# Four context pieces, and the context mixer moved to stand directly ahead of the state-space mixer

## What is computed

```
x   = macaron_ffn(x,   mod[:, 0:3],     *ffn1)      # main:    "ffn_4"
ctx = macaron_ffn(ctx, mod_ctx[:, 0:3], *ffn1)      # context: the pieces "ctx_a", "ctx_b", ...
h_ctx_f, h_ctx_b = context_states(ctx, ...)         # "ctx_mix"
x, _, _ = mix_sublayer(x, ..., h_ctx_f, h_ctx_b, ...)   # "ssd"
x = macaron_ffn(x, mod[:, 6:9], *ffn2)              # "ffn_5"
```

## Time and profile before

| | |
|---|---|
| median of 3 executions | 1648.93 us |
| the profiled execution's own time | 1650.2 us |
| its span, first to last instruction | 1648.4 us |
| TensorE busy | 1639.3 us (99%), 8804 matmuls |
| VectorE busy | 1249.4 us (76%) |
| ScalarE busy | 938.4 us (57%) |
| mean granted TensorE clock | 0.999 |

### The profile page before, as it was taken

How to read it: one execution, slowest core, us unless ns; L and a number is a source line. 1 busy time by engine, 2 the same in 40 slices (tenths; PEclk the granted TensorE clock), 3 DMA queues, 4 the chain that set the end, 5 groups by cost and what they waited for, 6 DMA issues and landing times.

```text
span 1648.4 us, 23158 instructions
## 1 busy us (share of the span) xinstructions
PE 1639.3 (99%) x8804; PEld 1417.2 (86%) x8804; DVE 1249.4 (76%) x1672; ACT 938.4 (57%) x1418; POOL 218.9 (13%) x368
## 2 busy tenths in 40 slices
PE   9999999999999999999999999999999999999998
PEld 7888889888888888888888888889888889988887
DVE  6888776788978877688788878779665669986564
ACT  6655567655565554565456546557655558664543
POOL 1100100001414000014005010122001012310000
PEclk9999999999999999999999999999999999999999
DMA  8977553687868687757658788674566545357551
GB/s 283 340 269 254 169 184 119 238 297 263 270 209 280 233 311 256 258 185 236 211 181 287 256 281 284 212 236 146 182 226 238 203 134 198 107 186 237 187 196 64
DMA packets 105342, 366.89 MB, mean 223 GB/s; under 512 B 13840, under 2 KB 14352, under 8 KB 105232
## 3 DMA queue, kind: packets, MB, share of 16 engines
q1 hardware_dynamic: 92736, 334.73, 59.6%
q0 software_dynamic: 12352, 30.61, 5.7%
q10 hardware_dynamic: 144, 0.07, 0.0%
HBM read 357.95 MB, written 2.17 MB: 218 GB/s over the span
## 4 chain that ended last, share of the span: by engine, by line
PE 91%; DVE 4%; DMA 2%; ACT 1%; issue 1%; SPq 0%; DVEq 0%; POOLq 0%; POOL 0%; ACTq 0%
PE dn L650 29%; PE gu L605 13%; PE tp L605 13%; PE gu L561 11%; PE gu L612 7%; PE tp L612 7%; PE dn L576 3%; DMA raw<-in_weights 2%; DVE w_lo L1958 1%; PE gu L589 1%; PE tp L589 1%; PE dn L605 1%; DVE w_lo L1951 1%; PE dn L561 1%; PE dn L612 1%
## 5 line engine op out<-in xcount | busy, mean ns | idle before, releaser
L1958 DVE TENSOR_TENSOR w_lo<-raw,w_hi 128x1024 fp32r<-128x1024 f32 x518 | 631.1, 1232 | 286.3 <-ACT w_hi L1261 283.5
L1261 ACT ACTIVATE w_hi<-raw 128x1024 fp32r<-128x1024 f32 x520 | 547.1, 1055 | 439.7 <-PE gu L612 153.4
L650 PE MATMUL dn<-w_hi,actT_hi 128*128 128x512 f32 x616 | 240.7, 391 | 0.0
L650 PE MATMUL dn<-w_hi,actT_lo 128*128 128x512 f32 x616 | 239.8, 389 | 0.0
L650 PE MATMUL dn<-w_lo,actT_hi 128*128 128x512 f32 x616 | 239.8, 389 | 0.0
L605 PE MATMUL tp<-hT,w_hi 128*128 128x512 f32 x928 | 232.2, 391 | 0.0
L605 PE MATMUL gu<-hT,w_hi 128*128 128x512 f32 x944 | 225.2, 389 | 0.3 <-DVE hT L1966 0.3
L561 PE MATMUL gu<-w_hi,hT 128*128 128x512 f32 x672 | 209.4, 393 | 0.9 <-DVE w_lo L1951 0.5
L605 PEld LDWEIGHTS gu<-hT,w_hi 128*128 128x128 f32 x944 | 177.0, 188 | 37.2 <-DVE hT L1966 0.6
L605 PEld LDWEIGHTS tp<-hT,w_hi 128*128 128x128 f32 x928 | 170.5, 188 | 32.9
L561 PEld LDWEIGHTS gu<-w_hi,hT 128*128 128x128 f32 x672 | 124.4, 188 | 27.5 <-DVE hT L1966 1.3
(11 more groups left out here) (367 smaller groups left out, 2028.0 us busy)
## 6 DMA issues: line engine op xcount, KB each, us to landing
raw<-in_weights SPq DMA_DIRECT2D x561, 512.0 KB, 4.4
arena<-in_ada_w SPq DMA_DIRECT2D x72, 512.0 KB, 4.4
post_row<-in_post_rows POOLq DMA_DIRECT2D x10, 512.0 KB, 6.4
pre_row<-in_pre_rows POOLq DMA_DIRECT2D x10, 512.0 KB, 7.6
arena<-xn POOLq DMA_DIRECT2D x160, 32.0 KB, 4.2
mod_row<-mod POOLq DMA_DIRECT2D x9, 512.0 KB, 9.7
shift_row<-mod POOLq DMA_DIRECT2D x5, 512.0 KB, 9.9
arena<-ctx_turned POOLq DMA_DIRECT2D x4, 512.0 KB, 9.1
```

The lines of the kernel that those rows point to most:

```text
L650: m = pe.matmul(dn[:, t, c], a[:, k, :], w[:, r, c], start=start and q == 0, stop=stop and q == 2)
L1261: act.activation(o, i, ACT.Copy, **kw).then_inc(done, 1)
L1958: dve.tensor_tensor(w_lo[:, r, :], raw[:, n % RAW, :], w_hi[:, r, :].bitcast(F32), ALU.subtract).then_inc(lo_ready, 1)
```

## The change

The context's feed-forward steps are split 3, 2, 3, 3 over four pieces; the fourth, ctx_d, stands between ffn_3 and ffn_4, where ctx_mix stood, and ctx_mix now stands between ffn_4 and ssd. `FED` reaches to ssd, so the inputs of ffn_4 and of ssd are turned by VectorE and transfers. ffn_4 ends with a step by column. ffn_4's input is scaled, normalised and block-turned in ctx_d, ssd's in ctx_mix. The rest of the context's states is done within ssd's first 8 slots. In a piece of two steps the second tile of the last activations is copied before the next phase's input. The arena's tiles are laid out anew, and the "ada" products spread otherwise. The diff, cut to what is spoken of:

```diff
-PIECE_STEPS = [4, 3, 4]
+PIECE_STEPS = [3, 2, 3, 3]
@@ phases
-          ("ctx_mix", 11), ("ffn_4", SLOTS_FFN), ("ssd", 31), ("ffn_5", SLOTS_FFN)]
+          ("ctx_d", 6 * PIECE_STEPS[3]), ("ffn_4", SLOTS_FFN), ("ctx_mix", 11), ("ssd", 31), ("ffn_5", SLOTS_FFN)]
-EARLY = [s for s in range(PIECE_A, FFN_4 + 1)]
-FED = [s for s in EARLY if s != FFN_4]
+FED = list(range(PIECE_A, SSD + 1))
-ADA_PLAN = [..., (PIECE_A, range(2, 4), 2),
-            (FFN_2, range(1, STEPS), 2), (PIECE_C, range(2, 4), 2), (FFN_3, range(1, 7), 2), (FFN_3, range(9, 10), 1)]
+ADA_PLAN = [..., (PIECE_A, range(2, 3), 2),
+            (FFN_2, range(1, STEPS), 2), (PIECE_C, range(2, 3), 1), (FFN_3, range(1, 10), 2)]
@@ TensorE, ctx_mix
-                    if p == 3:
-                        pe.wait_ge(dt_z, 1)
-                        transposed(s + 1, 0)
-                        pe.wait_ge(conv_done, 2)
-                        transposed(s + 1, 1)
                 log_decays(0)
                 context_x_tokens(0)
@@ TensorE, ssd
-                opening(s, n0, lambda t: None, lambda group: pe.wait_ge(wide_ready, group + 1))
+                wide_group(0, 0, lambda half: pe.wait_ge(hT_lo_ready, 2 * TT * s + 1 + FEED[s].index((half, 0))))
+                context_x_tokens(1)
+                wide_group(0, 1)
+                context_b_tokens()
+                pe.wait_ge(wide_ready, 1)
+                wide_group(1, 0, lambda half: half_input_there(s, half))
+                context_states()
+                pe.wait_ge(wide_ready, 2)
+                wide_group(1, 1)
                 dt_slot(n0 + 8)
+                pe.wait_ge(state_ready, 2)
@@ ScalarE, end of a feed-forward phase
                     last_upper(0)
+                    if last == 1:
+                        last_upper(1)
                     fed_upper(s + 1, 0)
                     after_slots(end + 4, 1)
-                    last_upper(1)
+                    if last > 1:
+                        last_upper(1)
                     fed_upper(s + 1, 1)
@@ VectorE, a piece's gaps (ahead)
                         if (j, q) in ((0, 1), (1, 0)):
+                            if s + 1 in MOD_IN:
+                                in_scaled(s + 1, j)
                             normalised(s + 1, j)
                             turned_in_blocks(s + 1, j)
@@ VectorE, ctx_mix
-                rows_modulated(FFN_4)
+                rows_modulated(SSD)
                 for t in range(TT):
-                    in_scaled(FFN_4, t)
-                dve.wait_ge(ada_stored, 16 * 3)
-                dt_biased(0)
-                dt_softplus(0)
-                for t in range(TT):
-                    normalised(FFN_4, t)
+                    in_scaled(SSD, t)
+                    normalised(SSD, t)
+                    turned_in_blocks(SSD, t)
+                    if t == 0:
+                        dve.wait_ge(ada_stored, 16 * 3)
+                        dt_biased(0)
+                        dt_softplus(0)
@@ VectorE, ssd
-                opening(s, n0, lambda group, t: None, lambda t: None, lambda q: None)
+                dve.wait_ge(p_exp, 1)
+                then(dve.tensor_tensor(exp_p[:, :, :], exp_p[:, :, :], dt[:, :, :], ALU.mult))
+                dve.wait_ge(tok_ready, TT)
+                x_times(exp_p)
+                after_slots(n0, 8)
@@ GpSimd
+            reload(PIECE_D)
...
+            pre_roots(FFN_4)
+            blocks_moved(FFN_4)
...
+            pre_roots(SSD)
+            blocks_moved(SSD)
```

More of the change, by code:

```diff
@@ L108, in by_column @@
     last = STEPS_OF[s] - 1
-    return s + 1 in FED if j == last else s in EARLY if 0 <= j < 2 else 2 <= j < last
+    return s + 1 in FED if j == last else s in FED if 0 <= j < 2 else 2 <= j < last
 def step_slot(s, j):
@@ L122 @@
     _pres = [("pre", _s + 1, t) for t in range(TT)] if _s + 1 in NORMED else []
-    NORMS += _pres + _posts if _s + 1 in EARLY else [k for t in range(TT) for k in _posts[t:t + 1] + _pres[t:t + 1]]
+    NORMS += _pres + _posts if _s + 1 in FED else [k for t in range(TT) for k in _posts[t:t + 1] + _pres[t:t + 1]]
 NORM_N = {k: i + 1 for i, k in enumerate(NORMS)}
@@ L135 @@
 for _s in range(len(SUB)):
-    FIRST += [("open", _s, q) for q in range(2) if _s not in EARLY]
+    FIRST += [("open", _s, q) for q in range(2) if _s not in FED or _s == SSD]
     FIRST += [("gu", _s, 0) for q in range(1) if _s in FFNS and _s not in COLUMN_ENDS]
@@ L437, in in_bank @@
         def in_bank(s, t, half):
-            return gu[:, half, :] if t and s == FFN_4 else tp[:, half, :]
+            return tp[:, half, :]
         def in_half(s, t, half):
@@ L667, in out_proj @@
                         pe.wait_ge(mix_lo, parts[k][t])
-                        if t and i == len(order) - 2 and s + 1 not in EARLY:
+                        if t and i == len(order) - 2 and s + 1 not in FED:
                             transposed(s + 1, 0)
@@ L1482, in ffn @@
                             act_upper(j - 1)
-                        if s == FFN_4 and j == 0:
-                            context_x_tokens()
                         after_slots(n, 1)
@@ L1827, in ssd @@
                 dt0, x0, s0 = n0 + 8, n0 + 9, n0 + 15
-                opening(s, n0, taken, lambda t: None)
+                act.wait_ge(first_tok, FIRST_N["open", s, 0])
+                taken(0, 0)
+                context_x_tokens()
+                act.wait_ge(first_tok, FIRST_N["open", s, 1])
+                taken(1, 0)
+                context_b_tokens()
+                after_slots(n0, 3)
+                act.wait_ge(slot_used, n0 + 4)
+                taken(0, 1)
+                after_slots(n0 + 3, 1)
+                context_states()
+                after_slots(n0 + 4, 3)
+                act.wait_ge(slot_used, n0 + 8)
+                taken(1, 1)
+                after_slots(n0 + 7, 1)
                 dt_turning(1, dt0)
@@ L2279, in ffn @@
                     for half in range(2):
-                        last_lower(half)
+                        if last > 1 or half == 0:
+                            last_lower(half)
+                        if last == 1 and half == 0:
+                            last_lower(1)
                         for t in range(TT):
```

119 lines of the change are left out of this document (50 added, 69 removed).

## The result

The changed kernel takes 1661.02 us (median of 5 runs, 1657.47 to 1661.15); the kernel before, beside it, 1649.33 us. The ratio of the means of these runs is 1.0065 (10.7 us), with a 95% interval of 1.0054 to 1.0076; the medians differ by 11.7 us, as the median of the changed kernel stands near its slowest run. It is slower. The forecast was 1657.0 us. The profiled execution took 1661.15 us, with a span of 1659.4 us. Waits in the profile's own list are 0.1 to 0.2 us shorter.

The account below looks back on a forecast made before the run. TensorE, busy 99% of the span, was taken to bound the kernel. Work off -4.55, piece b's seam +6.6 and ctx_mix +4.4 gave 1655.4 us by the median; +1.6 for the clock made 1657.0 us, range 1651.0 to 1661.0.

Parts of the forecast that it names:

- the two forecast waits: TensorE waits ahead of sc behind two-step piece b, +6.6 us for the seam, and ahead of ctx_mix's x tokens, 4.4 us.
- one of its own signs: Prediction is wrong if a wait over 1 us stands anywhere else, above all in ssd's opening or piece d.
- Work taken off TensorE: Fewer transposes for ffn_4's and ssd's inputs, ffn_4's last step by column, and an old seam delay gone: -4.55 us.
- ctx_mix: VectorE's two added block transposes delay its taps, so TensorE waits 4.4 us ahead of the x tokens.
- Piece b: Two-step piece ahead of sc: TensorE waits 1.15 us before last down products, some 4.6 behind the piece, then 0.9 more.
- the landing, at 4.8 us behind the last issue: In piece b, and reused in ctx_mix: last packet of the turned input lands 4.8 us after GpSimd's last issue.
- Piece d hidden: In three-step piece d the chain ends some 10 us early; two more scalings (1.2 us each) leave it hidden: 0 us.
- edits with no cost: Extra context reload, respread "ada" products and new arena layout cost nothing, covered by VectorE's 24% idle share.
- Piece c: In three-step piece c the input chain ends some 10 us before it is due; no wait forecast, 0 us.
- one fall of the two, +1.6: TensorE's clock falls behind one of the waits in piece b and ctx_mix, costing +1.6 us.
- the rival that followed this rule: Both waits stand and the clock falls in both: 1658.9 us, chance 0.20.

Follow-up runs that it names:

- x7: Changed kernel with the state-space mixer's modulated row formed in ffn_4's last step instead of in ctx_mix; 1657.38 us, ratio 1.0052.
- x9: Changed kernel with each of the two block transposes of the mixer's input cut to 32 columns (wrong input); 1655.91 us, ratio 1.0046.
- x13: Changed kernel with the mixer's input turned by TensorE in ctx_mix again, 16 transposes, no transfers for it; 1657.37 us, ratio 1.0051.
- x15: Changed kernel kept whole, its waits shortened by several reorderings, SyncE sharing sc's transfers, and nine unread products; 1650.96 us, ratio 1.0014.
- x4: Changed kernel with the context split 3, 3, 2, 3, so the two-step piece is c, not b; 1659.0 us, ratio 1.0057.
- x1: Changed kernel with GpSimd's multiply of the post row for ctx_d held until ctx_d's slots are used up; 1658.09 us, ratio 1.0053.
- x5: Changed kernel with SyncE issuing the 16 transfers of sc's second tile, placed too early in its order; 1669.95 us, ratio 1.0122.
- x6: Changed kernel with 18 unread products of 64 columns in TensorE's wait ahead of sc; 1659.36 us, ratio 1.0061.
- x14: x13 plus SyncE's transfers for sc, the held multiply, the earlier row, and piece b's last activations ahead of a slot; 1656.17 us, ratio 1.0041.

## Why the prediction came out as it did

The direction, the two forecast waits and the engines that they wait for were right. The time was at the very end of the range (1661.02 against 1661.0 us), 4.0 us over the forecast. By one of its own signs the forecast was wrong: a wait of more than 1 us stands elsewhere, in piece d, which it named, and in piece c. By its steps:

1. *Work taken off TensorE*, -4.55: measured -4.2. Right.
2. *ctx_mix*, +4.4: 4.6, with VectorE and TensorE as described. Shown by x7, x9 and x13. Right.
3. *Piece b*, 1.15 + 4.6 + 0.9: measured 1.3, 2.3 and 0.7. The mechanism was right; the mis-sized term is "the landing, at 4.8 us behind the last issue". The last packet came 1.4 us behind it, and the 1.3 us from there to the copy, which I had at nothing, made 2.7 (in x15 2.5). I had moved a time from a stretch in which weight loads filled the DMA engines (0.98 busy) to one in which they ran dry (0.18); x4 bears this out. How the time grows in between is open: in x15 the engines were 0.75 busy behind the last issue, which was SyncE's, and the copy was no later than in the change. I used 4.8 us in ctx_mix too, where it decided nothing.
4. *Piece d hidden*: its transfers were. But "edits with no cost" was judged by VectorE's idle share, and what failed is GpSimd's side: the change moved its multiply of `post_row` into the end of piece d, beside an instruction of VectorE that TensorE waits for. I had said that each queue which a step is moved past counts, and did not apply it here. 2.0 us and a fall of the clock; shown by x1.
5. *Piece c*: 1.6 us that I had at nothing. It goes with where a fetch of instructions falls; the cause stays open.
6. *The clock*: "one fall of the two, +1.6". Two falls, 3.2 us, in the profiled execution, one of them behind a wait I had not seen. Over the profiled executions of the changed kernel and its twelve variants: behind the nine waits of 3.5 us and more the clock fell each time, for 3.4 or 6.8 us (13.7 us with x5's 12.5); behind thirteen waits of 1.95 to 2.8 us it fell seven times; behind shorter ones never. The Trainium skill ("TensorE: Matmul & The Clock Gate", section "HAM oscillation — how this bites in real kernels") would have both long waits followed by slow products. For waits over 3.5 us the trace agrees, nine of nine, and the rival that followed this rule (a fall in every long wait) deserved more than 0.20; at waits near 2 us, where the clock fell about every second time, it decides nothing.

The two forecast waits were 2.0 us too large together, the two unforeseen ones are 3.6 us, and the clock cost 1.6 us more: the errors partly cancelled, and that the forecast was near is in part luck. Of its 4.0 us, 2.9 stand between the profiled executions; 1.1 come from the kernel before, whose profiled execution was 1.3 us above its median, while the changed kernel's was 0.1 us above.

## What to carry to other kernels

Where one engine is busy 99% of the time, work taken off it is worth having only if its replacement was already early. Ask for each moved step not only who is late, but which instruction of another engine it now runs beside. Do not carry the landing time of a transfer from one stretch to another without looking at how busy the DMA engines are in both. And a wait of the matrix engine has a second price, the half rate behind it: always here behind waits of 3.5 us and more, every second time behind those near 2 us. It cost 1.6 to 2.8 us of time each. Filling one with products that nothing reads kept the clock up behind it.

## What the runs showed of the hardware

- **VectorE's instructions with two inputs in SBUF and GpSimd's multiply exclude each other.** Such an instruction of VectorE (0.42 us) took 2.58 us beside GpSimd's multiply of two SBUF tiles; where VectorE was at such instructions when the multiply began, the multiply took 4.4 to 5.0 us instead of 2.4. The Trainium skill ("SBUF — State Buffer", section "Who interferes with whom") states that such a pair contends for a shared read port and that whoever issues first holds it for its whole instruction. The trace agrees in both orders. The multiply, begun at 1116.58, ends at 1119.42; VectorE's instruction, begun at 1117.12, ends 0.28 us later. In x7 VectorE goes from the activations on with two more runs of this kind, to 1117.80, and 2.40 us from there is 1120.20; the multiply ends at 1120.06. VectorE's additions at 1117.71, with one of their inputs in PSUM, take their usual 1.28 us beside it.
- **A late weight load goes with a fetch of instructions.** One packet of 16 KB, 0.9 to 1.9 us long on one of 16 DMA engines, and the 512 KB load in flight is used 2.0 to 2.7 us behind its end in twelve kernels. The page of the kernel after counts 111 packets of instructions; the 18 products added in x6 moved this one by 1.4 us. That the fetch is the cause was not tried.
- **The end of the program.** From the last packet of the output to the end of the span pass 0.75 us in twelve of the fourteen kernels, and 4.0 and 4.3 us in x13 and x14, with no engine at work. In x14 a packet of 8 KB of instructions starts at 1654.95, but that is 0.6 us behind the end of the span and so can't be what it waited for; x13 has none. The cause is open.
- **The spread.** The changed kernel's runs span 3.7 us, those of x15 2.6 us in 11 runs and those of the kernel before 1.2 us in 5. Falls of the clock behind waits near 2 us differ from execution to execution of much the same code, but they don't explain it alone: by the mean clock on record, the changed kernel's two runs at 1661.02 and 1661.15 us had 0.998 and 0.997, and its fastest, at 1657.47 us, had 0.997. The rest is open.
